# GpSimd applies the gate to each expert block's result, the expert sums start from x, and the final stage only normalises

## The reference

```python
def second_block(x, c, ...):
    ...
        h = modulate(rms_norm(x, norm2_g[l]), shift2, scale2)
        x = x + gate2[:, None, :] * hierarchical_moe(
            h, w_group[l], b_group[l], w_router[l], b_router[l],
            w_expert_gate[l], w_expert_up[l], w_expert_down[l])
    return rms_norm(x, final_norm_g)

def hierarchical_moe(...):
    ...
    def run_block(args):
        xb, e, wb = args
        a = jax.nn.silu(xb @ w_gate[e]) * (xb @ w_up[e])
        return (a @ w_down[e]) * wb[:, None].astype(xb.dtype)
    out = lax.map(run_block, (xg, blk_expert, slot_w.reshape(n_blocks, MOE_BLOCK)))
    y = jnp.zeros((T, D), h.dtype).at[slot_tok].add(out.reshape(cap, D))
```

## Time and profile before

| | us |
|---|---|
| median of three runs | 3200.73 |
| lowest, highest | 3199.76, 3204.96 |
| span of the profiled execution | 3202.1 |
| TensorE, VectorE, ScalarE, GpSimd busy | 2975.1, 1663.5, 1257.0, 778.8 |

### The profile page before, as it was taken

One profiled execution on the slowest core, in us unless ns is written; L12 is line 12 of the kernel. 1 busy time (PEld: TensorE's weight loads), 2 busy tenths in 40 slices (PEclk: granted clock), 3 DMA queues, 4 the chain that ended last, 5 costly groups with the idle time before them and its releaser, 6 DMA issues. The chain is left out here.

```text
span 3202.1 us, 39414 instructions
## 1 busy us (share of the span) xinstructions
PE 2975.1 (93%) x14311; PEld 2374.9 (74%) x14311; DVE 1663.5 (52%) x2590; ACT 1257.0 (39%) x1906; POOL 778.8 (24%) x388
## 2 busy tenths in 40 slices
PE   7999988999999999899999898999999897999993
PEld 4777775888778878677777787778768775888883
DVE  6444477522664326834444211443552326999996
ACT  4444343222222223434333311222221215899994
POOL 1111011444434434210000122121212121434440
PEclk9999998999999999999999999999999998999997
DMA  6100053222533336310000121011212214788773
GB/s 232 34 20 7 1 193 149 86 98 88 211 141 118 99 113 219 115 47 20 14 13 0 59 79 74 32 47 52 85 50 68 85 58 186 254 271 266 257 267 132
DMA packets 87734, 347.62 MB, mean 109 GB/s; under 512 B 21333, under 2 KB 27765, under 8 KB 76609
## 3 DMA queue, kind: packets, MB, share of 16 engines
q1 hardware_dynamic: 62568, 310.80, 26.6%
q0 software_dynamic: 17856, 16.85, 2.4%
q10 hardware_dynamic: 7192, 18.48, 1.6%
HBM read 377.94 MB, written 47.79 MB: 133 GB/s over the span
## 5 line engine op out<-in xcount | busy, mean ns | idle before, releaser
L3225 DVE TENSOR_TENSOR ex_g_lo<-ex_g_raw,ex_g_hi 128x1024 fp32r<-128x1024 f32 x188 | 220.8, 1215 | 1.9 <-ACT ex_g_hi L3164 1.9
L3164 ACT CAST ex_g_hi<-ex_g_raw 128x1024 fp32r<-128x1024 f32 x188 | 192.1, 1054 | 3.1 <-PE psum L3110 3.1
L1111 DVE TENSOR_TENSOR ff_gated<-psum,ff_silu 128x512 f32<-128x512 f32 x44 | 30.4, 691 | 312.6 <-PE psum L549 312.6
L495 POOL TENSOR_TENSOR ff0i_w_lo<-ff0i_w_raw,ff0i_w_hi 128x1024 fp32r<-128x1024 f32 x43 | 111.7, 2597 | 173.7 <-ACT ff0i_w_hi L455 133.8
L3108 PE MATMUL psum<-ex_g_hi,ex_x_hi 128*128 128x512 f32 x376 | 151.6, 403 | 0.0
L3109 PE MATMUL psum<-ex_g_lo,ex_x_hi 128*128 128x512 f32 x376 | 147.7, 393 | 0.0
L3110 PE MATMUL psum<-ex_g_hi,ex_x_lo 128*128 128x512 f32 x376 | 147.6, 393 | 0.0
L495 POOL TENSOR_TENSOR ff1i_w_lo<-ff1i_w_raw,ff1i_w_hi 128x1024 fp32r<-128x1024 f32 x43 | 111.0, 2582 | 142.1 <-ACT ff1i_w_hi L455 142.1
L549 PE MATMUL psum<-ff_h_hi,ff0i_w_hi 128*128 128x512 f32 x352 | 138.3, 393 | 6.5 <-ACT ff_h_hi L724 6.5
L3071 POOL DMA_INDIRECT expert_sums<-ex_o,token_ids x47 | 87.3, 1859 | 234.2 <-DMA expert_sums<-ex_o,token_ids 155.1
L549 PE MATMUL psum<-ff_h_hi,ff1i_w_hi 128*128 128x512 f32 x352 | 138.3, 393 | 4.0 <-POOLq L492 4.0
(11 more groups left out here) (569 smaller groups left out, 8137.5 us busy)
## 6 DMA issues: line engine op xcount, KB each, us to landing
ex_g_raw<-in_w_experts_gu_dram SPq DMA_DIRECT2D x32, 2048.0 KB, 7.8
ex_d_raw<-in_w_experts_d_dram SPq DMA_DIRECT2D x32, 1024.0 KB, 5.8
ff0i_w_raw<-in_ffn_in_dram SPq DMA_DIRECT2D x44, 512.0 KB, 3.2
ff1i_w_raw<-in_ffn_in_dram SPq DMA_DIRECT2D x44, 512.0 KB, 3.3
wom_w<-in_mod_w_dram SPq DMA_DIRECT2D x8, 2048.0 KB, 7.9
ff0o_w_raw<-in_ffn_out_dram SPq DMA_DIRECT2D x15, 704.0 KB, 4.9
ff1o_w_raw<-in_ffn_out_dram SPq DMA_DIRECT2D x15, 704.0 KB, 6.4
ga_w_raw<-in_w_merge_a_dram SPq DMA_DIRECT2D x16, 512.0 KB, 3.3
```

The costliest lines, as they stand in the source:

```text
L495: nc.gpsimd.tensor_tensor(w_lo[:, v % 2, :], w_raw[:, v % 2, :], w_hi[:, v % 2, :].bitcast(F32), ALU.subtract).then_inc(lo_made, 1)
L1111: nc.vector.tensor_tensor(gated[:], sums, silu[:], ALU.mult).then_inc(gated_made, 1)
L3164: nc.scalar.copy(cols(g_hi, n), cols(raw.g_raw[i % 3], n)).then_inc(q["g_hi_made"], 1)
L3225: nc.vector.tensor_tensor(cols(g_lo, n), cols(raw.g_raw[i % 3], n), cols(g_hi, n).bitcast(F32), ALU.subtract).then_inc(q["g_lo_made"], 1)
```

## The change

GpSimd multiplies `ex_o` in place with `gate_row` ahead of each adding transfer. `expert_sums` isn't filled with zeros in `mlstm`; SP stores the eight tiles of x there in `norm_route`, ahead of the stores of h. The final stage takes the sums as they are loaded: ScalarE squares them at once, VectorE only scales them, with four output buffers in place of two. GpSimd waits, after its first three gathers, until x is stored and `gate_row` is there. The core of the diff:

```diff
--- before.py
+++ after.py
-            sp.wait_ge(s_["zero_made"], 1)
-            for c in range(4):
-                sp.dma_start(sums_dram[:, c * (D // 4):(c + 1) * (D // 4)].rearrange("(i p) d -> p i d", p=P),
-                             zero[:].rearrange("p (o d) -> p o d", o=1).broadcast_to([P, NB, D // 4])).then_inc(s_["zeroed"], 16)
-            sp.wait_ge(s_["zeroed"], 64)
...
-            nc.gpsimd.memset(zero[:], 0.0).then_inc(s_["zero_made"], 1)
...
+            for i in range(NB):
+                sp.wait_ge(q["copied"], i + 1)
+                sp.dma_start(sums_dram[i * P:(i + 1) * P, :], x_tm[:, i, :]).then_inc(q["x_stored"], 16)
             for i in range(NB):
                 sp.wait_ge(q["copied"], NB + i + 1)
                 sp.dma_start(h_tm_dram[i * P:(i + 1) * P, :], tm[:, i % 2, :]).then_inc(t_stored[i % 2], 16)
...
         def store(i):
             pool.wait_ge(q["o_made"], i + 1)
+            nc.gpsimd.tensor_tensor(o[:, i % 2, :], o[:, i % 2, :], gate_r[:], ALU.mult).then_inc(q["gated"], 1)
+            pool.wait_ge(q["gated"], i + 1)
             if i >= 1:
                 pool.wait_ge(stored[1 - i % 2], 16 * ((i + 1) // 2))
             nc.gpsimd.indirect_dma_start(out=sums_dram[:, :],
...
+        pool.wait_ge(route["x_stored"], 16 * NB)
+        pool.wait_ge(route["gate_made"], 1)
         for i in range(N_BLK):
             if i + 3 <= LAST:
                 gather(i + 3)
...
         for i in range(NB):
             sp.wait_ge(self.made, i + 1)
-            sp.dma_start(self.out_dram[i * P:(i + 1) * P, :], self.y[:, i % 2, :]).then_inc(self.out_done[i % 2], 16)
+            sp.dma_start(self.out_dram[i * P:(i + 1) * P, :], self.y[:, i % 4, :]).then_inc(self.out_done[i % 4], 16)
...
         for i in range(NB):
-            act.wait_ge(self.link, 2 * i + 2)
+            act.wait_ge(self.e_in[i], 16)
             if i >= 1:
                 act.wait_ge(self.root, 2 * i)
-            nc.scalar.activation(self.sq[:], self.mixed[:, i % 2, :], ACT.Square, accum_out=st[:, 0, i:i + 1]).then_inc(self.summed, 1)
+            nc.scalar.activation(self.sq[:], self.e[:, i, :], ACT.Square, accum_out=st[:, 0, i:i + 1]).then_inc(self.summed, 1)
...
-        def mix(i):
+        def finish(i):
+            u = i % 4
             dve.wait_ge(self.e_in[i], 16)
-            if i >= 2:
-                dve.wait_ge(self.made, i - 1)
-            m = self.mixed[:, i % 2, :]
-            v.tensor_tensor(m, self.e[:, i, :], self.gate_r[:], ALU.mult).then_inc(self.link, 1)
-            dve.wait_ge(self.link, 2 * i + 1)
-            v.tensor_tensor(m, m, self.x_tm[:, i, :], ALU.add).then_inc(self.link, 1)
-            dve.wait_ge(self.link, 2 * i + 2)
...
             dve.wait_ge(self.root, 2 * i + 2)
             v.reciprocal(st[:, 3, i:i + 1], st[:, 2, i:i + 1]).then_inc(self.var, 1)
             dve.wait_ge(self.var, i + 1)
-            if i >= 2:
-                dve.wait_ge(self.out_done[u], 16 * (i // 2))
-            v.scalar_tensor_tensor(self.y[:, u, :], self.mixed[:, u, :], st[:, 3, i:i + 1], self.fin_r[:], ALU.mult, ALU.mult)\
+            if i >= 4:
+                dve.wait_ge(self.out_done[u], 16 * (i // 4))
+            v.scalar_tensor_tensor(self.y[:, u, :], self.e[:, i, :], st[:, 3, i:i + 1], self.fin_r[:], ALU.mult, ALU.mult)\
                 .then_inc(self.made, 1)
```

More of the change, by code:

```diff
@@ L2170, in end_dve, with mlstm @@
         self.chip.nc.vector.tensor_copy(self.g_cols[:].rearrange("p h n -> p (h n)"), self.chip.psum[:, 7, 0:XH * NB])
-def mlstm(chip, w_dram, wv_dram, conv_dram, rows_dram, g_cols, h_hi, h_lo, y, sums_dram, ahead):
+def mlstm(chip, w_dram, wv_dram, conv_dram, rows_dram, g_cols, h_hi, h_lo, y, ahead):
     nc = chip.nc
@@ L2205, in mlstm @@
     conv_all = chip.place("ml_conv_all", [P, 2 * XH, TAPS + 1], F32, FREE_AT + 16 * KIB + 512)
[L2206 to L2207 removed]
+    names = ("small_in", "rows_in", "vw_in", "v_hi_made", "v_lo_made", "hi_made", "lo_made", "later_made", "projected", "pre_made", "conved",
              "th_made", "qk_made", "v_summed", "v_ready", "gate_made", "staged", "padded", "scored", "decay", "cut", "weighted",
@@ L2621, in norm_route @@
 def norm_route(chip, gain, scale_col, shift_col, wr_dram, br_dram, h, h_tm_dram, x_tm, slot_w, more_rows, token_ids,
-               xg, raw, squares, gate_col, gate_r, weights, in_blk, of_blk, go_on):
+               sums_dram, xg, raw, squares, gate_col, gate_r, weights, in_blk, of_blk, go_on):
     nc = chip.nc
@@ L2663, in norm_route @@
              "logits", "turned", "copied", "exps", "link", "m_made", "before", "ranked", "hot", "placed",
-             "cleared", "ids", "diag_made", "spread", "gate_made")
+             "cleared", "ids", "x_stored", "diag_made", "spread", "gate_made")
     q = {n: chip.sem("ro_" + n) for n in names}
@@ L2719, in _ @@
                 raw.gather(nc.gpsimd, i, xg, h_tm_dram, token_ids)
-            go_on["pool"](pool)
+            go_on["pool"](pool, q)
         @block.tensor
@@ L2996, in load_more_d, with experts_programs @@
                                 bounds_check=NE * P - 1, oob_is_err=False).then_inc(self.more_d_in, 16)
-def experts_programs(chip, raw, xg, h_tm_dram, sums_dram, more_rows, token_ids, slot_w, weights, in_blk, of_blk, combine):
+def experts_programs(chip, raw, xg, h_tm_dram, sums_dram, gate_r, more_rows, token_ids, slot_w, weights, in_blk, of_blk, combine):
     nc = chip.nc
@@ L3021, in experts_programs @@
              "d_used", "silu_made", "a_made", "a_turned", "a_hi_made", "a_lo_made", "o_made",
-             "hot", "weighed")
+             "hot", "weighed", "gated")
     q = {n: chip.sem("ex_" + n) for n in names}
@@ L3060, in on_sp, with on_pool @@
         combine.on_sp(sp)
-    def on_pool(pool):
+    def on_pool(pool, route):
         def gather(i):
@@ L3280, with __init__ @@
 class Combine:
-    def __init__(self, chip, x_tm, gate_r, sums_dram, final_dram, out_dram):
-        self.chip, self.x_tm, self.gate_r, self.sums_dram, self.final_dram, self.out_dram = \
-            chip, x_tm, gate_r, sums_dram, final_dram, out_dram
+    def __init__(self, chip, sums_dram, final_dram, out_dram):
+        self.chip, self.sums_dram, self.final_dram, self.out_dram = chip, sums_dram, final_dram, out_dram
         self.fin_r = chip.place("co_final", [P, D], F32, FREE_AT + 14 * KIB)
         self.e = chip.place("co_e", [P, NB, D], F32, B_AT + 24 * KIB)
-        self.mixed = chip.place("co_mixed", [P, 2, D], F32, B_AT)
-        self.y = chip.place("co_y", [P, 2, D], F32, B_AT + 8 * KIB)
+        self.y = chip.place("co_y", [P, 4, D], F32, B_AT)
         self.sq = chip.place("co_sq", [P, D], F32, B_AT + 16 * KIB)
@@ L3292, in __init__ @@
         self.warm = chip.place("co_warm", [P, 1], F32, B_AT + 21 * KIB)
-        self.fin_in, self.ready, self.link, self.summed, self.var, self.root, self.made = \
-            (chip.sem("co_" + n) for n in ("fin_in", "ready", "link", "summed", "var", "root", "made"))
+        self.fin_in, self.ready, self.summed, self.var, self.root, self.made = \
+            (chip.sem("co_" + n) for n in ("fin_in", "ready", "summed", "var", "root", "made"))
         self.e_in = [chip.sem(f"co_e_in{i}") for i in range(NB)]
-        self.out_done = [chip.sem(f"co_out{u}") for u in range(2)]
+        self.out_done = [chip.sem(f"co_out{u}") for u in range(4)]
     def start_sp(self, sp):
@@ L3306, in on_sp @@
             sp.wait_ge(self.made, i + 1)
-            sp.dma_start(self.out_dram[i * P:(i + 1) * P, :], self.y[:, i % 2, :]).then_inc(self.out_done[i % 2], 16)
-        for u in range(2):
-            sp.wait_ge(self.out_done[u], 16 * NB // 2)
+            sp.dma_start(self.out_dram[i * P:(i + 1) * P, :], self.y[:, i % 4, :]).then_inc(self.out_done[i % 4], 16)
+        for u in range(4):
+            sp.wait_ge(self.out_done[u], 16 * NB // 4)
     def on_act(self, act):
@@ L3409, in two_blocks @@
         ahead = FirstWeights(chip, "gm", A["w_merge_m"], KD * P, gm_w[1], gm_w[2], raw=gm_w[0][:, 0, :])
-        steps, y_made = mlstm(chip, A["w_ml"], A["w_mlv"], A["conv"], decay_rows, g_cols, h[0], h[1], branch, sums, ahead)
+        steps, y_made = mlstm(chip, A["w_ml"], A["w_mlv"], A["conv"], decay_rows, g_cols, h[0], h[1], branch, ahead)
         merged = chip.place("merged", [P, KD, S], F32, X_AT)
@@ L3432, in two_blocks @@
         norm_route(chip, chip.gains[:, 5, :], 80, 72, A["w_route"], A["b_route"], whole, h_tm, x_tm, slot_w, more_rows,
-                   token_ids, xg, raw, squares, 88, gate_r, weights, in_blk, of_blk,
-                   experts_programs(chip, raw, xg, h_tm, sums, more_rows, token_ids, slot_w, weights, in_blk, of_blk,
-                                    Combine(chip, x_tm, gate_r, sums, A["final_gain"], A["out"])))
+                   token_ids, sums, xg, raw, squares, 88, gate_r, weights, in_blk, of_blk,
+                   experts_programs(chip, raw, xg, h_tm, sums, gate_r, more_rows, token_ids, slot_w, weights, in_blk, of_blk,
```

(1 more changed line is left out.)

5 lines of the change are left out of this document (removed).

## The result

The changed kernel takes 3240.79 us (median of four runs, 3237.10 to 3250.36), the kernel before 3200.88 (median of four runs, three of them those of the table above; 3199.76 to 3204.96): 1.0124 times as long, 95% interval 1.0104 to 1.0145. The forecast was 3246 us, range 3212 to 3267, slower with a chance of 0.88. The profiled execution has a span of 3242.3 us, 40.2 more than the one of before.

The account below looks back on a forecast made before the run. TensorE bounds the expert stage at 9.29 us a block, then a serial tail; VectorE would become the bound. Terms +54.5, +3.4, +1.2, +2.5 (+61.6) less 15.7 give +45.9 on 3200.7: forecast 3246 us, range 3212 to 3267.

Parts of the forecast that it names:

- up to the first ex_o, stores of x among it: Before the expert stage: x stores delay the h stores at most 1 us; taken as 0, at most 1.
- start of the expert stage: First adding transfer goes 3.4 us later, handed on through transfer, wait and gather: +3.4 us, bounds 2.4 to 4.5.
- 41 blocks, less the slack: Expert stage: GpSimd's product holds an ex_g_lo, 1.39 us more per block; 57.0 less VectorE's 2.5 us lead over TensorE: +54.5.
- last ex_d_lo: End of expert stage: the product of block 45 holds the last ex_d_lo: +1.2 us, bounds 0 to 1.2.
- last product, serial: End of expert stage: the last product lies serially between ex_o and the last adding transfer: +2.5 us.
- tail: Final stage: VectorE no longer sets the end, loads and stores of 8.39 MB do: -15.7 us, bounds 13 to 17.5.
- Hidden: Rival, expert stage: VectorE loses under 0.6 us per block, TensorE stays the bound: 3188 to 3191 us, chance 0.08.
- the clock: Rival, expert stage: TensorE's clock falls in the new pauses, some 4 of 41 blocks at 1.2 GHz: 3278 us, chance 0.04.
- beside ex_x_lo: Rival, expert stage: GpSimd's product always starts with ex_x_lo, 0.66 us more per block: 3215 us, chance 0.17.
- VectorE keeps its turn over several instructions: Other form of the 3215 us rival: GpSimd's product waits until VectorE reaches a PSUM reader; they share chance 0.17.

Follow-up runs that it names:

- e3: Changed kernel, but VectorE multiplies by the gate out of PSUM in place of ScalarE's copy, with no GpSimd product: 3207.89 us.
- e4: Changed kernel with GpSimd's product made twice per block, one after the other: 3340.68 us.
- e5: Changed kernel with GpSimd's product in two halves of 512 columns, the second held back to lie beside ex_x_lo: 3242.88 us.
- e6: Changed kernel with one wait ahead of GpSimd's whole product, so that it starts beside ex_x_lo: 3229.75 us.
- e9: As e6, with GpSimd issuing each gather of h rows one block earlier, ahead of the product: 3222.07 us.
- e11: Changed kernel, but VectorE multiplies columns 0 to 511 out of PSUM, GpSimd the rest beside ex_x_lo, gathers one block earlier: 3194.53 us.
- e12: As e11, but ex_x_lo goes ahead of the second ex_d_lo and GpSimd's half product starts as soon as ex_o is there: 3198.65 us.
- e10: Kernel before, with only the gathers issued one block earlier: 3193.06 us, 0.9985 of before.
- e7: Changed kernel with final-stage outputs written over the loaded sums, so no output waits for a store: 3244.08 us, tail 25.18 us.

## Why the prediction was right, and where its sizes were off

The mechanism of the blocks held: VectorE becomes the bound because it stands still until GpSimd's product is done. The start of the stage went otherwise than reckoned, and the near hit of the sum is in part luck. VectorE's own work takes 8.67 us a block (it shows as the period of the first blocks of before, where VectorE runs ahead). What each kernel adds to that, read from its own timeline, gives its period. As VectorE has no idle time in these blocks, the sum must come out; what it shows is which instruction is held, and that nothing else has grown:

| kernel | added to 8.67 us | sum | period measured |
|---|---|---|---|
| after | two ex_g_lo 4.14 - 2.35 | 10.46 | 10.47 |
| e3 | one pass, 1.13 | 9.80 | 9.80 |
| e4 | 6.35 - 2.35 | 12.67 | 12.67 |
| e5 | 0.19, and 2.30 or 3.03 less 1.21 | 9.95, 10.68 | 9.97, 10.69 |
| e6, e9 | two ex_g_lo 3.72 - 2.35 | 10.04 | 10.04 |
| e11 | half a pass 0.60, 2.61 - 2.34 | 9.54 | 9.53 |
| e12 | half a pass 0.60, and 0 or 2.66 - 1.21 | 9.27, 10.72 | 9.27, 10.72 |

The terms of the sum, in the profiled executions (ex_o's ends in both; together they make up the span's 40.2 us):

| term, us | forecast | measured |
|---|---|---|
| up to the first ex_o, stores of x among it | 0, at most 1 | +1.0 |
| start of the expert stage | +3.4 | 0.0 |
| 41 blocks, less the slack | +54.5 | +50.0 |
| last ex_d_lo | +1.2 | +1.1 |
| last product, serial | +2.5 | +2.4 |
| landing of the last adding transfer | 0 | +0.1 |
| tail | -15.7 | -14.4 |

- *The blocks.* 10.47 us instead of 10.68. The place was right, beside ex_a and then on an ex_g_lo. GpSimd starts 0.13 us ahead of ex_a, and the held ex_g_lo ends 1.08 us behind GpSimd's recorded end where it takes 1.21 alone, so VectorE loses 1.79 and not 1.99. By itself this would take 0.21 x 41 = 8.6 off the 54.5. Some 4 us came back: the slack of 2.5 is spent in the first four blocks and not in these 41, and the last of the 41 took 10.47 where it had been 8.41 before, 0.9 more than the other blocks lost.
- *The start.* This step failed. I carried the first adding transfer's delay of 3.4 us through to the end. That transfer is issued 5.6 us later, but the gather that the kernel before stalls on the earlier trace rows only 1.7 us later (2748.92 and 2747.23), and TensorE turns its rows at 2759.81 without a wait. The stall is gone; e10 shows that it is worth 3.8 us and hangs on when the gather is issued. In its place the first four blocks are longer, as VectorE is the bound there already (periods 8.67, 10.56, 10.88, 10.88): they take 41.0 us, as before with its stall, and e10 takes 37.2. So the 0.0 of the table is 3.8 less and 3.8 more, a coincidence. A delay ahead of the place where the bound moves isn't added to the new bound's time, but the blocks ahead of that place have to be counted.
- *The tail.* -14.4 instead of -15.7. That transfers bind it is shown by e7. By their landings the stores follow the loads, as I had it: the last load lands at 3231.91, store 0 at 3233.14, 9 us after its issue and 1.24 behind that load. What was too short is the loads: the seven behind the first land over 11.0 us and not 9.1, with two steps of 2.5 and 2.0 us among steps of 1.2 to 1.4. The first of these ends 0.6 us after the first store's issue, so it isn't the stores alone; the cause is open. The DMA engines ran at 378 GB/s over the stretch, where I had taken the peak of 422. Besides, a step of my sum was written wrongly: 3180.7 + 0.2 + 1.3 + 1.3 is 3183.5. The 3185.9 is store 3 and four more stores at 1.3, which is how it came about. The 358 GB/s of the Trainium skill (SBUF — State Buffer, summary of rules for kernel authors), which I had set aside, would by the estimate made from it have given about 12 back: the 14.4 of the trace lies between the two.
- *The stores of x.* The h stores land later behind them, and ScalarE waits 2.4 us for a buffer of ro_tm. At most 0.5 us of the 1.0 in the table is theirs: the other 0.5 is there before the first of them is issued (SP issues the weights of L2979 at 2640.21, before at 2639.71 as L2983; the first store of x follows at 2648.47). Only the trace says so; no run took it alone.
- *The sum.* The terms miss by +1.0, -3.4, -4.5 and +1.3 us; that the whole misses by only 5.7 of 45.9 owes something to their signs.
- *The rivals.* Hidden (3188 to 3191) is refuted by the period; the clock stayed at 1.00 in the stage; "beside ex_x_lo" (3215) didn't come by itself, but forced in e9 it gave 3222.07. "VectorE keeps its turn over several instructions" came once in full, at the first product (4.51 us); why only there wasn't tried. The trace's 4.14 against 2.35 us agrees with the rule of the Trainium skill (SBUF — State Buffer, section Who interferes with whom) that such a pair excludes each other and the later one blocks fully. That the later one is the one that waits doesn't hold for every recorded start: 27 cases in e5 and nine in e12, told of below, went the other way.

## What to carry to other kernels

Before giving an idle GpSimd an elementwise product, count what VectorE, with which it shares the work, has to spare in a period, and which of its instructions need both inputs from SBUF: the product costs VectorE its whole length but for what lies beside PSUM readers, here 1.8 of 2.4 us. Where VectorE is nearly full, a pass on VectorE out of PSUM, or half of one with the other half on GpSimd next to a PSUM reader, is cheaper (9.80 and 9.53 against 10.47 us a block). An overlap that is set up by a wait on one queue holds only if nothing variable stands ahead of it there, and what stands behind it (here the gathers) must be issued first.

## What the hardware showed that was not expected

- **A product right behind a DMA issue can overtake.** In the blocks of e5 and e12 shown above, the VectorE instruction is recorded as started 0.63 and 0.27 us ahead of GpSimd's product, and still ends 1.09 us after it. All such cases (27 in e5, nine in e12) have GpSimd's issue of a weight gather end within 0.04 us of the product's start, and a head start of VectorE of 0.24 to 0.66 us. The issue alone isn't enough: six products of the changed kernel stand as close behind one, VectorE's head start there is 0.81 to 1.00 us, and none overtakes. Nor does such an issue hold VectorE by itself: none of the 282 ex_g_lo and ex_d_lo of before takes over 1.29 us. Whether VectorE is held already while the issue runs is open, and no run varied the head start.
- **Issues that stretch.** The issue of an adding transfer on GpSimd takes 1.77 us at the median in e11 and 1.79 in the changed kernel. Ahead of each of e12's nine late products it takes 3.67 to 4.17, and the gather's issue behind it 2.9 where 1.4 is common, and this is what makes the product late. What stretches them wasn't tried.
